# MoE blocks of 32 tokens on four 32-column strips in a two-layer encoder trunk

## The chip, the cores and the metric

The kernel is one program on one core of a Trainium2 chip. The metric is device time in microseconds (us) from launch to end. All arithmetic is float32. Engines: TensorE (PE: matmuls; PEld: its weight loads), VectorE (DVE), ScalarE (ACT), GpSimd (POOL), SyncE (SP, which issues most DMAs here).

## What is computed

The reference is a trunk of two layers on 256 tokens of width 1024: a convolution mixer, then an attention mixer. After each mixer comes a layer norm and a mixture of experts (MoE). The change touches only the MoE, and so the rest is left out here. The reference's MoE, cut:

```python
logits = (t @ router_w) + router_b                     # t: 256 x 1024 tokens, 16 experts
probs = softmax(logits).reshape(N, 4, 4)               # 4 groups of 4 experts
g_sel = argmax(top_k(probs, 2)[0].sum(-1))             # one group for a token
w_top, i_top = top_k(probs of that group, 2)           # two experts of it
w_top = w_top / w_top.sum(-1)
...
y_block = (silu(xb @ w_gate[e]) * (xb @ w_up[e])) @ w_down[e]
...
out[token] += weight * y_block[slot]
```

Each of the three matrices of an expert is 1024 x 1024, 4 MB, so an expert has 12 MB, and the two layers 384 MB.

## The kernel before

The expert weights stream through a ring of eight slots of 2 MB. A slot holds half of a matrix (512 rows by 1024 columns); in the text a *half* is such a piece. `load` (L295 and on, its `dma_start` is L303) on SyncE issues half number `index` into slot `index % 8`, and waits before that until the semaphore `half_free` says that half `index - 8` has been released. `load_experts` issues six halves an expert, in the order gate 0, gate 1, up 0, up 1, down 0, down 1. The 16 experts are walked in four turns of a hardware loop; its body has the code of four experts (`UNROLL`), so that slot numbers are fixed in it.

The router (`moe` of VectorE) finds for each token its two experts and its place in each one's list, and for each expert the number of blocks, `blocks_i`. A block is `SLOTS` = 64 places of an expert's list. The engines read that number into a register and branch by it. Each engine has its own copy of the walk, and they meet at semaphores that count blocks (`n_pe`, `n_dve`, `n_act`).

A block goes through these steps:

- VectorE builds a 0/1 matrix G (tokens by slots, L1170) and the same with router weights, GW (L1173).
- TensorE gathers: `sum_x` (L747) multiplies G with the tokens `hs`. The 64 slots fill 64 columns of the array, so columns 0 to 511 of the tokens go on one strip of 64 columns and the rest on the other (`tile_position`), and the result is 128 x 512.
- ScalarE copies it (L455), `turn_x` transposes it (L759), VectorE copies it to XT (L1179).
- `product` (L770) multiplies with gate, then with up, then (in `down`) with the down matrix: 16 matmuls of 128x64 by 128x512 each time, alternating between two strips.
- ScalarE applies silu to the gate product (L459), as soon as that is there and while the up product runs; VectorE multiplies by up (L1184).
- `down` transposes the hidden block (L783) and GW (L789), ScalarE copies the first (L463), VectorE the second (L1188), then comes the down product; ScalarE copies its result (L466).
- `combine` (L801) multiplies with GW and adds to the sums of all tokens in PSUM banks 0 to 3.

`expert` writes three bodies: a loop for all but the last two blocks, the last block, and, within conditionals between the last one's steps, the block before it. Two buffers of everything let these two go side by side. `sum_x` of the following expert stands ahead of `combine`. Halves are released in pairs, with the first matmul after the product that used them, in the last block only. A shortened view of the last part:

```python
n = pe.snap(n_pe) + 1
turn_x(0, n)
with pe.If(blocks > 1): ...                      # block 1: sum_x, turn_x
product(gate_w, ...)                             # and block 1's
product(up_w, ..., frees 2)                      # and block 1's
down(0, n, down_w, turn, 2)                      # and block 1's, with its combine
sum_x(0, following, 2)
combine(0, n, 0)
```

## Time and profile before

| | us |
|---|---|
| runs, median of 3 | 1681.42 |
| runs, lowest and highest | 1673.98, 1688.25 |
| profiled execution, span | 1682.1 |
| first product of layer 0's experts to the last combine's end | 281.43 to 805.73 |
| the same of layer 1 | 1107.12 to 1662.11 |
| weights moved by SyncE's queue | 490.90 MB |

The runs are three timed executions of the same program. The profile is one more execution with the hardware profiler on; its times are what the sums are made from. The span is from its first to its last instruction. Every fp32 matmul stands in the profile as two records, each with its weight load; transposes are one record each. A busy share says how much of the time an engine had an instruction in work, not that it set the end; the chain of waits follows the work back from the last instruction.

### The profile page before, as it was taken

How to read it: one execution, taken by the hardware profiler on the slowest of the kernel's cores; microseconds unless marked ns; L12 is line 12 of the kernel's file. 1: busy time of each engine (PE TensorE's matmuls, PEld its weight loads, DVE VectorE, ACT ScalarE, POOL GpSimd, SP SyncE). 2: the span in 40 equal slices, each digit the busy share in tenths (PEclk: the TensorE clock that was granted, in tenths of full speed). 3: DMA queues.
4: the chain of work that ended last, by engine and by line, in shares of the span. 5: the costliest groups of instructions: out<-in, count | busy, mean ns of one | idle time of the engine just before them, and what ended most of it. 6: DMA issues, size and time to landing. Idle time of an engine off the chain costs nothing.

```text
span 1682.1 us, 16133 instructions
## 1 busy us (share of the span) xinstructions
PE 1416.4 (84%) x6244; PEld 628.7 (37%) x6245; DVE 342.6 (20%) x821; ACT 258.9 (15%) x426; POOL 56.8 (3%) x89
## 2 busy tenths in 40 slices
PE   2795889996998798798799999789969897997996
PEld 0574534332333233233367565333323332332332
DVE  0199242101001001001601331510101110100103
ACT  0104201121011121121100211111111111121121
POOL 0290000000000000000000000000000000000000
PEclk8797988998999899899899857689989998998997
DMA  9816666999599999999952502149967778999991
GB/s 338 337 74 277 250 252 263 409 408 371 200 350 409 360 409 408 381 409 413 411 206 101 200 1 84 66 165 408 408 247 276 303 279 320 381 408 405 383 408 45
DMA packets 119596, 497.12 MB, mean 296 GB/s; under 512 B 6396, under 2 KB 6396, under 8 KB 111270
## 3 DMA queue, kind: packets, MB, share of 16 engines
q1 hardware_dynamic: 115404, 490.90, 74.1%
q10 hardware_dynamic: 3930, 4.09, 0.8%
q8 instruction: 123, 2.02, 0.5%
q14 instruction: 11, 0.09, 0.0%
q0 software_dynamic: 128, 0.02, 0.0%
HBM read 493.94 MB, written 1.05 MB: 294 GB/s over the span
## 4 chain that ended last, share of the span: by engine, by line
PE 78%; DVE 11%; issue 6%; ACTq 3%; ACT 2%; DMA 1%; DVEq 0%; SPq 0%
PE PS L770 45%; PE PS L669 5%; PE PS L747 4%; PE PS L801 4%; DVE work L1248 3%; PE PS L687 3%; PE PS L900 2%; PE PS L604 2%; PE PS L759 1%; PE PS L975 1%; PE PS L885 1%; PE PS L978 1%; DVE work L1179 1%; PE PS L783 1%; ACTq L422 1%
## 5 line engine op out<-in xcount | busy, mean ns | idle before, releaser
L770 PE MATMUL PS<-ring,work 128*64 128x512 f32 x3360 | 750.4, 603 | 55.7 <-DVE work L1179 34.9
L770 PEld LDWEIGHTS PS<-ring,work 128*64 128x64 f32 x3360 | 253.3, 139 | 510.3 <-issue 489.5
L1184 DVE TENSOR_TENSOR work<-work,PS 128x512 f32<-128x512 f32 x35 | 24.1, 688 | 515.5 <-PE PS L770 515.5
L1179 DVE COPY work<-PS 128x512 f32<-128x512 f32 x35 | 24.2, 692 | 360.9 <-PE PS L759 360.9
L669 PE MATMUL PS<-ring,hT 128*128 128x512 f32 x192 | 84.8, 603 | 4.1 <-ACT hT L526 3.6
L747 PE MATMUL PS<-hs,work 128*64 128x512 f32 x280 | 73.4, 644 | 9.6 <-DVE work L1173 9.6
L1248 DVE SCALAR_TENSOR_TENSOR work<-work,colv 128x256 f32<-128x256 f32 x150 | 77.3, 576 | 1.1
L604 PE MATMUL PS<-ring,crep 128*32 128x512 f32 x448 | 62.5, 707 | 17.7 <-DMA ring<-in_w_ada_dram 15.9
L759 PE MATMUL PS<-ident,work 128*128 128x128 f32 x140 | 25.7, 312 | 59.3 <-issue 55.8
L801 PE MATMUL PS<-work 64*128 64x512 f32 x280 | 69.6, 615 | 3.6 <-ACT work L466 3.6
L459 ACT ACTIVATE work<-PS 128x512 f32<-128x512 f32 x35 | 20.9, 598 | 326.8 <-PE PS L770 326.8
L463 ACT ACTIVATE work<-PS 128x512 f32<-128x512 f32 x35 | 20.9, 597 | 268.4 <-PE PS L783 268.4
L885 PE MATMUL PS<-hT,ring 128*128 128x256 f32 x256 | 58.2, 392 | 4.7 <-ACT hT L432 4.7
L466 ACT ACTIVATE work<-PS 128x512 f32<-128x512 f32 x35 | 20.9, 598 | 255.7 <-PE PS L770 255.7
L687 PE MATMUL PS<-hT,ring 128*128 128x256 f32 x256 | 55.8, 380 | 1.9 <-DVE hT L1038 1.9
L669 PEld LDWEIGHTS PS<-ring,hT 128*128 128x128 f32 x192 | 36.9, 193 | 50.3 <-issue 49.6
L885 PEld LDWEIGHTS PS<-hT,ring 128*128 128x128 f32 x256 | 50.5, 198 | 12.4 <-ACT hT L432 5.1
L687 PEld LDWEIGHTS PS<-hT,ring 128*128 128x128 f32 x256 | 48.5, 190 | 9.4 <-DVE hT L1038 2.2
L759 PEld LDWEIGHTS PS<-ident,work 128*128 128x128 f32 x140 | 16.4, 153 | 89.5 <-issue 63.0
L455 ACT ACT_TABLE_LOAD x32 | 41.1, 1283 | 40.2 <-issue 30.6
L900 PE MATMUL PS<-work,hs 128*128 128x256 f32 x124 | 30.1, 408 | 19.4 <-DVE work L1234 19.4
L783 PE MATMUL PS<-ident,work 128*128 128x128 f32 x140 | 22.1, 281 | 27.6 <-DVE work L1184 27.6
(197 smaller groups left out, 895.0 us busy)
## 6 DMA issues: line engine op xcount, KB each, us to landing
ring<-in_w_gate_dram SPq DMA_DIRECT2D x64, 2048.0 KB, 16.8
ring<-in_w_up_dram SPq DMA_DIRECT2D x64, 2048.0 KB, 13.2
ring<-in_w_down_dram SPq DMA_DIRECT2D x64, 2048.0 KB, 16.4
ring<-in_w_ada_dram SPq DMA_DIRECT2D x24, 2048.0 KB, 20.3
ring<-in_w_pw_dram SPq DMA_DIRECT2D x6, 2048.0 KB, 41.3
ring<-in_w_ada_kv_dram SPq DMA_DIRECT2D x4, 2048.0 KB, 14.9
ring<-in_w_kvf_dram SPq DMA_DIRECT2D x4, 2048.0 KB, 21.9
ring<-in_w_q_dram SPq DMA_DIRECT2D x2, 2048.0 KB, 24.0
```

What stands on the lines that cost most here:

```text
L455: act.activation(Xg[b], PS[:, X_BANK[b], :], ACT.Copy).then_inc(X_copied, 1)
L604: last = pe.matmul(PS[32 * q:32 * q + 32, bank, :], crep[:, k, :], quarter(index + j, kk, 2)[:, q * BANK:(q + 1) * BANK], start=(k == 0), ...
L669: last = pe.matmul(PS[:, banks + 2 * t + q, :], hT[:, k, t * P:(t + 1) * P], quarter(index + h, kk, KH)[:, q * BANK:(q + 1) * BANK], start ...
L687: last = pe.matmul(PS[:, banks + f // 2, (f % 2) * SEQ:(f % 2 + 1) * SEQ], quarter(index + h, kk, KH)[:, f * P:(f + 1) * P], hT[:, k, :], ...
L747: last = pe.matmul(PS[SLOTS * q:SLOTS * (q + 1), X_BANK[b], :], G[b][:, t, :], hs[:, t, q * BANK:(q + 1) * BANK], start=(t == 0), stop=(t ...
L759: last = pe.transpose(PS[:, XT_BANK[b], cc * P:(cc + 1) * P], Xg[b][:, cc * P:(cc + 1) * P], ident[:, :])
L770: last = pe.matmul(PS[SLOTS * q:SLOTS * (q + 1), bank, :], stationary[:, kk, SLOTS * h:SLOTS * (h + 1)], quarter(load + h, kk, KH)[:, q * ...
L801: last = pe.matmul(PS[:, 2 * t + q, :], GWT[b][SLOTS * q:SLOTS * (q + 1), t * P:(t + 1) * P], yb[b][SLOTS * q:SLOTS * (q + 1), :], start=F ...
L885: last = pe.matmul(PS[:, f, g * SEQ:(g + 1) * SEQ], quarter(L_PW1 + j, kk, 2)[:, g * D + f * P:g * D + (f + 1) * P], hT[:, k, :], start=(k ...
L900: last = pe.matmul(PS[:, f, 0:SEQ], diag(n), U[:, f, j:j + SEQ], start=(j == 0), stop=(j == TAPS - 1))
L1179: dve.tensor_copy(XT[b].rearrange("p c s -> p (c s)"), PS[:, XT_BANK[b], :]).then_inc(XT_copied, 1)
L1248: ins = dve.scalar_tensor_tensor(out=CV[:, fc, :], in0=U[:, fc, j:j + SEQ], scalar=colv[:, fc, j:j + 1], in1=CV[:, fc, :], op0=ALU.mult, o ...
```

## The change

A block has 32 slots. The array has four strips of 32 columns, and the steps are laid out over them:

- `gate_up` puts gate's two halves of the columns on strips 0 and 1 and up's on strips 2 and 3, so that one pass of 32 matmuls does both. Gate lies in partitions 0 to 63 of bank 4, up in 64 to 127. Silu starts when both are done.
- `sum_x` gathers on four strips, a quarter of the token's columns each: 8 matmuls of 256 columns. Two transposes replace four.
- `down` puts even and odd row blocks of the down matrix on different strips; their two partial sums are added by `combine`, whose matmuls keep their shape, as GW holds its weights four times over.
- The gather of the next block (of the same expert or of the next) lies inside a block: `sum_x` behind `gate_up`, `turn_x` behind the transposes of the hidden block. The first gather of a layer stands ahead of the loop.
- There is one buffer of each, and one body per block. An expert with several blocks runs all but the last in a loop, and then the last.
- The loads of an expert go gate 0, up 0, gate 1, up 1, down 0, down 1. In the last block the first pair is released in the middle of `gate_up`, the second at the first transpose of GW, and the down halves one by one, in mid-product and with `combine`.
- The number of blocks is found with one comparison against eight limits and a sum.

```diff
+SLOTS = 32
+STRIPS = 4
 RING = 8
...
-        X_BANK, XT_BANK = (7, 5), (6, 4)
-        GATE_BANK, UP_BANK = (4, 6), (5, 7)
-        HT_BANK, GWT_BANK, DOWN_BANK = (4, 6), (5, 7), (5, 7)
+        GU_BANK, X_BANK, GWT_BANK, HT_BANK, DOWN_BANK = 4, 5, 6, 7, 4
...
-                        for m, w in enumerate((gate_h, up_h, down_h)):
-                            for h in range(2):
-                                load(index + 6 * i + 2 * m + h,
-                                     w[bass.ds(e, 1), h].rearrange("o p k f -> (o p) k f"), turn * TURN)
+                        for m, (w, h) in enumerate(((gate_h, 0), (up_h, 0), (gate_h, 1), (up_h, 1),
+                                                    (down_h, 0), (down_h, 1))):
+                            load(index + 6 * i + m,
+                                 w[bass.ds(e, 1), h].rearrange("o p k f -> (o p) k f"), turn * TURN)
...
+                    act.activation(Xg, PS[:, X_BANK, 0:QUART], ACT.Copy).then_inc(X_copied, 1)
+
+                def gate(n):
+                    act.wait_ge(gate_up_done, n)
+                    act.activation(hh[64:P, :], PS[0:64, GU_BANK, :], ACT.Silu).then_inc(sil_ready, 1)
...
                 act.wait_ge(routed, l + 1)
+                take_x(act.snap(n_act) + 1)
...
+                    with act.If(blocks > 1):
+                        with act.Fori(0, blocks - 1):
                             n = act.snap(n_act) + 1
-                            take_x(0, n)
-                            gate(0, n)
-                            take_result(0, n)
+                            gate(n)
+                            take_x(n + 1)
+                            take_result(n)
                             act.reg_add(n_act, n_act, 1)
...
-                        for q in range(2):
-                            last = pe.matmul(PS[SLOTS * q:SLOTS * (q + 1), X_BANK[b], :], G[b][:, t, :],
-                                             hs[:, t, q * BANK:(q + 1) * BANK], start=(t == 0),
+                        for q in range(STRIPS):
+                            last = pe.matmul(PS[SLOTS * q:SLOTS * (q + 1), X_BANK, 0:QUART], G[:, t, :],
+                                             hs[:, t, q * QUART:(q + 1) * QUART], start=(t == 0),
...
+                def gate_up(n, load, turn, frees):
+
+                    pe.wait_ge(XT_copied, n)
+                    for h in range(2):
+                        arrived(load + 2 * h, turn)
+                        arrived(load + 2 * h + 1, turn)
+                        for kk in range(KH):
+                            q, cc = 2 * h + kk // 2, kk % 2
+                            for strip in range(STRIPS):
+                                half = strip % 2
+                                last = pe.matmul(PS[SLOTS * strip:SLOTS * (strip + 1), GU_BANK, :],
+                                                 XT[:, cc, SLOTS * q:SLOTS * (q + 1)],
+                                                 quarter(load + 2 * h + strip // 2, kk, KH)[:, half * BANK:(half + 1) * BANK],
+                                                 start=(h == 0 and kk == 0), stop=(h == 1 and kk == KH - 1),
+                                                 tile_position=(0, SLOTS * strip), skip_group_check=True)
+                        if h == 0 and frees:
+                            last.then_inc(half_free, 2)
+                    last.then_inc(gate_up_done, 1)
+
+                def turn_gw_await_hh(n, frees):
+
+                    pe.wait_ge(GW_built, n)
+                    for t in range(TT):
+                        if t == TT - 1:
+                            pe.wait_ge(hh_ready, n)
+                        last = pe.transpose(PS[:, GWT_BANK, t * P:(t + 1) * P],
+                                            GW[:, t, :, :].rearrange("p r s -> p (r s)"), ident[:, :])
+                        if frees and t == 0:
+                            last.then_inc(half_free, 2)
+                    last.then_inc(GW_turned, 1)
+
+                def turn_hh(n):
...
                     for cc in range(KH):
...
+                        last = pe.transpose(PS[:, HT_BANK, cc * 2 * SLOTS:(cc + 1) * 2 * SLOTS],
+                                            hh[64:P, cc * P:(cc + 1) * P], ident[64:P, 64:P])
+                    last.then_inc(hh_turned, 1)
...
+                def down(n, load, turn, frees):
+
+                    pe.wait_ge(hhT_copied, n)
                     for h in range(2):
...
+                            for half in range(2):
+                                strip = 2 * half + kk % 2
+                                last = pe.matmul(PS[SLOTS * strip:SLOTS * (strip + 1), DOWN_BANK, :],
+                                                 hhT[:, kk, SLOTS * h:SLOTS * (h + 1)],
+                                                 quarter(load + 4 + h, kk, KH)[:, half * BANK:(half + 1) * BANK],
+                                                 start=(h == 0 and kk < 2), stop=(h == 1 and kk >= KH - 2),
+                                                 tile_position=(0, SLOTS * strip), skip_group_check=True)
+                        if h == 0 and frees:
+                            last.then_inc(half_free, 1)
+                    last.then_inc(down_done, 1)
...
+                                             GWT[64 * q:64 * (q + 1), t * P:(t + 1) * P],
+                                             yb[64 * q:64 * (q + 1), :], start=False, stop=False,
...
                             if frees and t == q == 0:
-                                last.then_inc(half_free, frees)
...
+                                last.then_inc(half_free, 1)
...
+                def expert(load, turn, blocks, closes_turn):
+
+                    with pe.If(blocks > 1):
+                        with pe.Fori(0, blocks - 1):
                             n = pe.snap(n_pe) + 1
-                            turn_x(0, n)
-                            product(gate_w, turn, GATE_BANK[0], XT[0], gate_done, 0)
-                            product(up_w, turn, UP_BANK[0], XT[0], up_done, 0)
-                            down(0, n, down_w, turn, 0)
-                            sum_x(0, n + 1, 0)
-                            combine(0, n, 0)
+                            gate_up(n, load, turn, False)
+                            sum_x(n + 1)
+                            turn_gw_await_hh(n, False)
+                            turn_hh(n)
+                            turn_x(n + 1)
+                            down(n, load, turn, False)
+                            combine(n, False)
                             pe.reg_add(n_pe, n_pe, 1)
...
+                    gate_up(n, load, turn, True)
                     if closes_turn:
                         with pe.If(turn < E // UNROLL - 1):
-                            sum_x(0, following, 0)
-                        combine(0, n, 2)
+                            sum_x(n + 1)
                     else:
-                        sum_x(0, following, 2)
-                        combine(0, n, 0)
+                        sum_x(n + 1)
+                    turn_gw_await_hh(n, True)
+                    turn_hh(n)
+                    if closes_turn:
+                        with pe.If(turn < E // UNROLL - 1):
+                            turn_x(n + 1)
+                    else:
+                        turn_x(n + 1)
+                    down(n, load, turn, True)
+                    combine(n, True)
+                    pe.reg_add(n_pe, n_pe, 1)
 
                 pe.wait_ge(routed, l + 1)
-                sum_x(0, pe.snap(n_pe) + 1, 0)
+                first = pe.snap(n_pe) + 1
+                sum_x(first)
+                turn_x(first)
...
-                link(dve.tensor_scalar(r_n[:, :], cnt, float(SLOTS), 1.0, ALU.is_gt, ALU.add))
-                for m in range(2, SEQ // SLOTS):
-                    dst = r_n if m < SEQ // SLOTS - 1 else blocks_i
-                    link(dve.scalar_tensor_tensor(out=dst[:, :], in0=cnt, scalar=float(m * SLOTS), in1=r_n[:, :],
-                                                  op0=ALU.is_gt, op1=ALU.add))
+                NB = SEQ // SLOTS
+                limits = slot1[0:1, SLOTS - 1:SLOTS - 1 + SEQ].rearrange("o (m s) -> o m s", s=SLOTS)[:, :, 0]
+                link(dve.tensor_tensor(r_over[:, :, :], cnt.unsqueeze(2).to_broadcast([1, E, NB]),
+                                       limits.unsqueeze(1).to_broadcast([1, E, NB]), ALU.is_gt))
+                link(dve.tensor_reduce(r_n[:, :], r_over[:, :, :], AX.X, ALU.add))
+                link(dve.tensor_scalar(blocks_i[:, :], r_n[:, :], 1.0, None, ALU.max))
...
+                def build_G(e, end_slot):
+
                     for t in range(TT):
-                        dve.tensor_scalar(G[b][:, t, :], slots, r_pos[:, t, bass.ds(e, 1)], None, ALU.is_equal)
+                        last = dve.tensor_scalar(G[:, t, :], slots_of(end_slot), r_pos[:, t, bass.ds(e, 1)], None,
+                                                 ALU.is_equal)
+                    last.then_inc(G_built, 1)
...
+                def build_GW(e, end_slot):
...
+                        last = dve.tensor_scalar(GW[:, t, :, :], slots, r_pos[:, t, bass.ds(e, 1)],
+                                                 r_wn[:, t, bass.ds(e, 1)], ALU.is_equal, ALU.mult)
+                    last.then_inc(GW_built, 1)
...
+                    dve.tensor_tensor(hh[64:P, :], hh[64:P, :], PS[64:P, GU_BANK, :], ALU.mult).then_inc(hh_ready, 1)
...
+                build_G(0, SLOTS)
+                build_GW(0, SLOTS)
+                take_xT(dve.snap(n_dve) + 1)
...
+                    with dve.If(blocks > 1):
+                        with dve.Fori(0, blocks - 1) as j:
                             n = dve.snap(n_dve) + 1
-                            build(0, e, (j + 1) * SLOTS)
-                            take_xT(0, n)
-                            times_up(0, n)
-                            take_weights(0, n)
+                            build_G(e, (j + 2) * SLOTS)
+                            times_up(n)
+                            take_weights(n)
+                            take_xT(n + 1)
+                            build_GW(e, (j + 2) * SLOTS)
                             dve.reg_add(n_dve, n_dve, 1)
...
+                    with dve.If(e < E - 1):
+                        build_G(e + 1, SLOTS)
+                    times_up(n)
+                    take_weights(n)
+                    with dve.If(e < E - 1):
+                        take_xT(n + 1)
+                        build_GW(e + 1, SLOTS)
                     dve.reg_add(n_dve, n_dve, 1)
```

How this moves instructions, first on TensorE: the last block of an expert, with what stands in conditionals between its steps, before (L759 and L747 the gather, L770 the products; "x" is the number of instructions):

```order
L759 MATMUL PS<-ident,work 128x128 x4
L826 COMPARE_AND_BRANCH
L744 REGISTER_ALU
L747 MATMUL PS<-hs,work 64x512 x4
L759 MATMUL PS<-ident,work 128x128 x4
L826 UNCONDITIONAL_BRANCH
L587 ISA
L770 MATMUL PS<-ring,work 64x512 x16
L830 COMPARE_AND_BRANCH
L770 MATMUL PS<-ring,work 64x512 x16
L830 UNCONDITIONAL_BRANCH
L770 MATMUL PS<-ring,work 64x512 x16
```

and the same place now (L768 `gate_up`, L744 the gather of the next block, L783 GW, L792 the hidden block, L754 the next gather's transposes, L804 `down`, L819 `combine`):

```order
L840 ISA
L584 ISA
L768 MATMUL PS<-ring,work 32x512 x32
L741 REGISTER_ALU
L744 MATMUL PS<-hs,work 32x256 x8
L783 MATMUL PS<-ident,work 128x128 x2
L792 MATMUL PS<-ident,work 128x64 x4
L754 MATMUL PS<-ident,work 128x128 x2
L804 MATMUL PS<-ring,work 32x512 x16
L819 MATMUL PS<-work 128x512 x4
L856 ISA
```

The conditional copies between the products are gone, one pass of 32 matmuls stands where two of 16 stood, and the gather lies between it and `down`. The loop ahead of it, now run for every block but the last:

```order
L830 ISA
L584 ISA
L768 MATMUL PS<-ring,work 32x512 x32
L741 REGISTER_ALU
L744 MATMUL PS<-hs,work 32x256 x8
L783 MATMUL PS<-ident,work 128x128 x2
L792 MATMUL PS<-ident,work 128x64 x4
L754 MATMUL PS<-ident,work 128x128 x2
L804 MATMUL PS<-ring,work 32x512 x16
L819 MATMUL PS<-work 128x512 x4
L838 ISA
L829 COMPARE_AND_BRANCH
```

Its backward branch stands behind `combine`. The same on SyncE, the six loads of the first expert of a turn (REGISTER_ALU computes the value to wait for), before:

```order
L303 DMA ring<-in_w_gate_dram 128x4x1024
L301 REGISTER_ALU
L303 ISA
L303 DMA ring<-in_w_gate_dram 128x4x1024
L301 REGISTER_ALU
L303 DMA ring<-in_w_up_dram 128x4x1024
L301 REGISTER_ALU
L303 DMA ring<-in_w_up_dram 128x4x1024
L301 REGISTER_ALU
L303 DMA ring<-in_w_down_dram 128x4x1024
L301 REGISTER_ALU
L303 DMA ring<-in_w_down_dram 128x4x1024
```

and now:

```order
L305 DMA ring<-in_w_gate_dram 128x4x1024
L303 REGISTER_ALU
L305 DMA ring<-in_w_up_dram 128x4x1024
L303 REGISTER_ALU
L305 ISA
L305 DMA ring<-in_w_gate_dram 128x4x1024
L303 REGISTER_ALU
L305 DMA ring<-in_w_up_dram 128x4x1024
L303 REGISTER_ALU
L305 DMA ring<-in_w_down_dram 128x4x1024
L303 REGISTER_ALU
L305 DMA ring<-in_w_down_dram 128x4x1024
```

The first up half has moved ahead of the second gate half; their number and size are the same. On ScalarE silu now stands ahead of the copy of a gather, which is that of the next block; it has half the partitions.

## Rows read from the trace of the kernel before

**Rows 1.** The head of the page: span, busy time and share of each engine.

```profile
span 1682.1 us, 16133 instructions
...
PE 1416.4 (84%) x6244; PEld 628.7 (37%) x6245; DVE 342.6 (20%) x821; ACT 258.9 (15%) x426; POOL 56.8 (3%) x89
```

**Rows 2.** Chain of waits in order of time: start us, us, engine, line, records.

```profile
281.43 15.67 PE PS L770 x64
...
414.67 29.38 PE PS L770 x128
...
497.82 13.98 PE PS L770 x64
514.13 7.09 PE PS L770 x32
521.22 1.72 PE PS L747 x8
522.93 1.92 PE PS L801 x8
526.48 13.98 PE PS L770 x64
...
553.65 9.29 issue
565.21 15.72 PE PS L770 x64
...
803.74 1.99 PE PS L801 x8
...
1107.12 15.67 PE PS L770 x64
...
1660.12 1.99 PE PS L801 x8
```

**Rows 3.** Groups by line: busy us, mean ns | idle before; VectorE's product, then GW.

```profile
L1184 DVE TENSOR_TENSOR work<-work,PS 128x512 f32<-128x512 f32 x35 | 24.1, 688 | 515.5 <-PE PS L770 515.5
...
L1173 DVE TENSOR_SCALAR work<-slot,r_pos,r_w 128x64 f32 x140 | 34.3, 311 | 0.0
```

**Rows 4.** Windows: busy of PE, PEld, DVE, ACT, POOL; then clock, DMA share, GB/s.

```profile
308.00:396.00 88.00, 80.07 (x376) 29.14 (x374) 9.34 (x27) 16.59 (x20) 0.00 (x0) 1.00 1.03 408
420.00:430.00 10.00, 10.00 (x50) 3.42 (x46) 0.00 (x0) 0.60 (x1) 0.00 (x0) 1.00 0.01 2
36.00:60.00 24.00, 12.10 (x56) 4.78 (x56) 6.84 (x7) 0.00 (x0) 0.00 (x0) 0.64 1.03 408
```

**Rows 5.** Timeline, TensorE's four-strip adaLN product, full and low clock.

```profile
176.18 7.07 PE L604 MATMUL PS<-ring,crep 128*32 128x512 f32 x64
...
29.80 3.42 PE L604 MATMUL PS<-ring,crep 128*32 128x512 f32 x16 [3.93 <-DMA ring<-in_w_ada_dram]
```

**Rows 6.** Timeline, hand-offs around down, combine, and a router product.

```profile
483.23 0.69 DVE L1184 TENSOR_TENSOR work<-work,PS 128x512 f32<-128x512 f32 x1 [14.48 <-PE PS L770]
...
484.06 0.63 PE L783 MATMUL PS<-ident,work 128*128 128x128 f32 x4 [0.95 <-DVE work L1184]
...
484.73 0.60 ACT L463 ACTIVATE work<-PS 128x512 f32<-128x512 f32 x1 [7.84 <-PE PS L783]
484.95 0.42 DVE L1188 COPY work<-PS 128x256 f32<-128x256 f32 x1 [1.03 <-PE PS L789]
...
461.65 1.99 PE L801 MATMUL PS<-work 64*128 64x512 f32 x8 [0.69 <-ACT work L466]
...
255.66 2.52 PE L713 MATMUL PS<-rw,hT 128*128 128x16 f32 x21 [0.78 <-DVE hT L1038]
```

**Rows 7.** SyncE's issues by time, then issue to landing for 425 to 470 us.

```profile
270.31 3.08 SPq L303 DMA_DIRECT2D ring<-in_w_gate_dram  x2
...
431.20 0.92 SPq L303 DMA_DIRECT2D ring<-in_w_up_dram  x2
...
DMA to landing us min/median/max: 7.9/10.8/13.8
```

162 lines of the change are left out of this document (42 added, 120 removed).

## The prediction

> **What bounds the kernel now.** I read the page's head first: a span of 1682.1 us, and TensorE with something to do for 84% of it [rows 1]. That share does not say which stage TensorE holds back, so the chain of waits in order of time comes next [rows 2]. It shows the two MoE stages, 281 to 805.7 us (803.74 plus 1.99) and 1107 to 1662.1 us, built almost wholly of TensorE work. A one-block expert repeats every 28.66 us (497.82 to 526.48): 13.98 for gate and up, 7.09 for down, 1.72 for the next gather, 1.92 for the combine, and 3.95 of hand-offs and transposes. After every fourth expert the loop turns back and the chain has 9.29 us of "issue"; from the last combine to the next gate product pass 11.56 us (553.65 to 565.21) where it is 1.63 otherwise (524.85 to 526.48), so a turn costs 9.8 to 9.9; I take 9.8. The first product after it takes 15.72 instead of 13.98, 1.7 more. There are 35 blocks over the 32 experts of the two layers [rows 3].
>
> The DMA side is nearly as full. Where one-block experts run undisturbed the queue moves 408 GB/s at a share of 1.03 and TensorE's clock is 1.00; inside the two-block expert at 414.67 the queue moves 2 GB/s, since all ring slots wait to be released [rows 2, 4]. A half of a weight is 2.097 MB, so it costs 2.097/0.408 = 5.14 us and an expert's six 30.8 us. That is more than 28.66: TensorE keeps its pace only because the DMA queue catches up in the turns. So a faster block cannot gain more than the DMA's slack.
>
> **The new block.** Count its matmuls: 32 for gate and up, 16 for down, 8 narrow ones for the gather, 4 for the combine, 8 transposes (16, 16, 16, 4, 4, and 10 before). Each fp32 matmul is two records. On two strips 64 records take 13.98 us; on four 32-column strips the adaLN product does 64 in 7.07 [rows 2, 5]. So gate with up is 7.0 and down 3.5. The combine stays 1.92.
> Between gate_up and down: ScalarE's silu 0.60, VectorE's product 0.69, three hand-offs of 0.1 to 0.15 (483.23 + 0.69 to 484.06, say), then five short transposes at 0.63 for four, and a copy of 256 columns, 0.42 on VectorE, with 0.15 around it [rows 6]: 1.65 + 0.75 + 0.57 = 3.0, and I take 3.1 because ScalarE copies the next gather ahead of it. The gather of the next block and its two transposes lie in this gap. The gather is 16 records of half the columns: 0.9 us at the adaLN rate, 2.0 at the rate of the small router products, which 21 records at 2.52 us show [rows 6]; silu and product cover 1.65, so it adds nothing or up to 0.4. What is late there if it is longer is the transpose of the hidden block. Down to combine is 0.69, with a copy of 0.60 between [rows 6]. In sum 7.0 + 3.1 + 3.5 + 0.7 + 1.9 = **16.2 us per block**; bounds 15.7 (less cover needed) and 18.
>
> The number of blocks follows from the reference's router on its drawn inputs. Of at most 32 tokens each, layer 0 has one block per expert but three for expert 4 and two for experts 5, 6, 10, 11, 15: 23 for 17 now. Layer 1 has the same with three for expert 6: 24 for 18. The two stages take 524 + 555 = 1079 us now. TensorE's work in them falls to 47 x 16.2 and six turns of 9.8, 820 us, under the 987 us that 192 halves cost. The stages become bound by the DMA queue, and by what the ring makes it wait.
>
> **The sum.** Rules: a half lands 5.14 us after the one before. If the ring was full, 3.6 us pass between the release and the start: two halves issued into an idle queue landed 7.9 and 13.8 us after their issue, that is 2 x 5.14 + 3.5 [rows 7]. An expert's first release comes 3.5 us into its last block, 12.7 before its end. The ring has room for two halves beyond an expert in work. After a turn or a long wait a block takes 1.7 more.
> Layer 0 begins its first product at 280.5 (281.43 now [rows 2]; the first gather is shorter by 1 to 2.5). Halves 6 and 7, issued at 270.31, land by 288.1 [rows 7]. Half 23 lands at 288.1 + 16 x 5.14 = 370.3, expert 3 ends 4.4 later (half of down, copy, combine), and with the turn expert 4 begins at 384.5. Its three blocks cost 3 x 16.2 + 2 x 1.7 + 3.1 (its last halves are late) + 5 for the loop back, explained below: it ends at 444.7 and first releases at 432.0. The last two halves with room, up to 31, landed at 411.5: the DMA pauses 20.5 us. From then no pause: half 95 lands at 432.0 + 3.6 + 64 x 5.14 = 764.5, and what is left is 4.4 and one whole block: **785.1 against 805.7, -20.6**.
> Layer 1 (in its own times of now) starts with a full ring at 1105, first release 1110.2. Half 23 lands at 1113.8 + 82.2 = 1196.0; expert 4 runs 1210.2 to 1270.4, releases at 1257.7; expert 5 takes 32.4, expert 6 48.6 + 5 + 1.7, to 1358.1, releases at 1345.4, a second pause of 22.4. Half 95 lands at 1345.4 + 3.6 + 52 x 5.14 = 1616.3, the end is 20.6 later: **1636.9 against 1662.1, -25.2**. Sum -45.8. The same rules, given the blocks of now, end at 806.4 and 1661.9.
> The profiled execution has 1682.1 us, the median of the runs 1681.4: 1682.1 - 45.8 = 1636.
>
> **Edits costed at nothing.** The order gate, up, gate, up of the loads and the earlier releases (two halves in mid-product) are in the rules. G and GW are built by VectorE in four steps of about 0.31 us [rows 3] while TensorE does 7 us of products. The load of silu's table stands on ScalarE ahead of silu, after the block's last copy, beside combine and products. The test of the block count is one step shorter. What stands outside the MoE is untouched.
>
> **What the trace does not show: the loop inside an expert.** Now its body never runs, since no expert has three blocks of 64. Its backward branch will be taken three times. The nearest row is the turn, 9.3 us [rows 2]; the lower end is nothing, since the body is about an eighth of a turn. I take 5, the middle. At nothing the total is -66, at 9.3 it is -33. All of it is on the path: TensorE is late then, and the ring full.
> The Trainium skill, "Runtime: NRT & Kernel Launch", section "Instruction fetch mechanics", says that a taken branch out of the pages at hand stalls for a fetch. The turn's 9.29 us agree; no row here shows whether the short jump leaves those pages. By that rule read strictly the sum is the -33 case, 1649.
>
> **Rivals.**
> A. Loop backs at full price, as above: 1649. For: it is the nearest row. Against: the body is short.
> B. No loop-back cost: 1616.
> C. The block is longer than 16.2, through a hand-off that I cannot see. One us more on each block costs 29 us, since it delays the multi-block experts and lengthens the pauses: 1665, no change to speak of. For: in the new gap ScalarE and VectorE work in turns, with branches between their steps. Against: most of these branches fall under products.
> D. Slower: every run of the loop body, 15 in all, stalls TensorE as the turn does, not only the three loop backs. Place: between the blocks of an expert, with its six slots held. At 9.3 each the total is +108, 1790; it is slower than now from about 2 us each, with 1.7 more for the clock. Against: the 128 records of products at 414.67, half of them from conditional bodies, run now in one piece of 29.38 us [rows 2].
> E. The clock stays low. In 36 to 60 us, where TensorE waits for weights, the granted clock is 0.64 and 16 records of the four-strip product take 3.42 us instead of 1.77 [rows 4, 5]. One-block experts at half speed need 16.2 + 12.4 = 28.6 us and stay under 30.8, so it costs nothing there. If it stayed so through the first 25 us after each wait the total is +2; a return after 3 to 14 us leaves -46. The row at 565.21 shows it back within the product.
> The Trainium skill, "TensorE: Matmul & The Clock Gate", section "HAM oscillation — how this bites in real kernels", says that a kernel whose matmuls wait for each slice of weights starts every slice at the low clock. By it the one-block experts show a clock well under 1.00, and the sum stays, as they have the time.
> F. The change does nothing, because the DMA was the bound already: 1682. Against: without pauses layer 0 would end at 288.1 + 452.3 + 20.6 = 761, 45 us before it does now.
>
> **How the numbers follow.** My forecast with its own spread (rate 5.00 to 5.28 us per half: -55 to -23; loop back 0 to 9.3) 55%, B's end 15%, A 10%, C 11%, D 5%, E 3%, F 1%. Range 1598 (B with the faster rate and 15.8 us per block) to 1675. A measurement of this kernel can tell about 1% (17 us) from no change. Faster by over 1%: forecast, B, A, half of C, 0.82. Within 1%: the rest of C, F, part of E, 0.10. Slower: D and what is left, 0.08.
>
> **What would show it.** Right: 64 gate-up records in 7.0 us, 32 down in 3.5, blocks in multi-block experts every 16 to 17 us; waits of TensorE on the ring's DMA, which are absent now; the DMA at 408 GB/s but for one gap in layer 0 and two in layer 1 of about 20 us; TensorE's clock and busy share lower. Wrong: no waits on the ring, blocks of 18 us or more, issue gaps between an expert's blocks, or a rate per record over 0.12 us at the full clock.

## The result, and where the time went

| | before | after |
|---|---|---|
| runs, median | 1684.84 (the three of the earlier table and one more) | 1628.93 (4 runs, 1627.07 to 1653.75) |
| ratio | | 0.968, 95% interval 0.9623 to 0.9736 |
| profiled execution, span | 1682.1 | 1625.2 |
| first gate product of layer 0 | 281.4 | 283.4 |
| layer 0's experts, first product to last combine | 524.3 | 513.6 |
| from there to layer 1's first gate product | 301.4 | 279.4 |
| layer 1's experts | 555.0 | 528.9 |
| from there to the end | 20.0 | 19.9 |

The prediction was 1636; the kernel measured 1628.93, faster by 3.2%. The ratio is formed without the run of 1653.75, in which TensorE's granted clock was lower than in the other three (0.863 against 0.876 to 0.887). The stages of the two profiles add up to 56.9 us: +2.0 ahead of layer 0, -10.7 in it, -22.0 between the two, -26.1 in layer 1. So the experts' stages gave -36.8, where -45.8 was predicted (3 of it from earlier starts), and -22.0 came from a stretch whose code is the same in both kernels and where nothing was predicted. The total was met by luck: one term was too large and one was missing.

The head of the page of after, which answers to [rows 1], and its shares of the chain:

```profile
span 1625.2 us, 19834 instructions
...
PE 1247.7 (77%) x7990; PEld 530.1 (33%) x7991; DVE 351.9 (22%) x835; ACT 244.7 (15%) x457; POOL 56.7 (3%) x89
...
PE 47%; DMA 33%; DVE 8%; issue 4%; ACT 3%; ACTq 3%; SPq 2%; DVEq 0%
```

There are more instructions, TensorE's share falls from 84% to 77%, and a third of the chain is now DMA. (In the chain a DMA piece is a load from its issue to its landing. TensorE works through most of that time and waits only for its end.) The chain of waits of after in order of time, which answers to [rows 2] (start us, us, engine, line, records):

```profile
283.38 9.12 PE PS L768 x64
...
309.12 24.86 DMA ring<-in_w_up_dram
...
349.71 25.41 DMA ring<-in_w_down_dram
...
409.69 1.99 PE PS L819 x8
411.68 7.05 PE PS L768 x64
421.31 3.69 PE PS L804 x32
425.67 1.99 PE PS L819 x8
427.66 7.00 PE PS L768 x64
436.40 19.42 DMA ring<-in_w_down_dram
...
460.50 7.00 PE PS L768 x64
...
509.30 4.85 issue
...
532.93 10.30 issue
...
794.95 1.99 PE PS L819 x8
...
1076.33 8.55 PE PS L768 x64
...
1603.27 1.99 PE PS L819 x8
```

The three-block expert of layer 0 shows the new block undisturbed: 64 records of gate and up in 7.05 us, down in 3.69, the combine in 1.99, and 15.98 from block to block (411.68 to 427.66). The backward jump of the loop inside an expert lies ahead of the second of its three blocks, and the chain has no gap at it: 409.69 + 1.99 is 411.68. Nor has it one where the loop is left: 425.67 + 1.99 is 427.66. Elsewhere the chain runs through the loads, 19 to 25 us each, of up and of down halves. TensorE itself waits for a few microseconds at a time. Its waits for expert weights over the whole execution (us in total, times, longest):

```profile
PE PS L768 <- DMA ring<-in_w_up_dram: 139.8, 29, 6.1
...
PE PS L804 <- DMA ring<-in_w_down_dram: 14.5, 19, 2.0
```

That is 154 us in 48 waits, where the experts of the kernel before have none.

Windows of after, beside [rows 4] (busy of PE, PEld, DVE, ACT, POOL; then clock, DMA share, GB/s): the one-block experts of layer 0, the last blocks of the three-block expert, and 50 us of layer 1's attention.

```profile
308.00:396.00 88.00, 55.89 (x382) 18.11 (x374) 7.60 (x21) 9.70 (x15) 0.00 (x0) 0.84 1.03 408
415.00:430.00 15.00, 13.87 (x124) 4.66 (x120) 2.44 (x7) 3.23 (x5) 0.00 (x0) 1.00 0.03 10
...
941.00:991.00 50.00, 50.00 (x260) 30.85 (x253) 23.13 (x88) 12.56 (x53) 0.00 (x0) 0.95 0.16 61
```

In the first row the queue is as full as before (408 GB/s, share 1.03) and TensorE busy for 56 of 88 us where it was 80. In the second the ring is full of weights in use and the queue stands still.

**The stretch between the layers.** Of the -22.0 us, 19.4 lie in layer 1's attention, from the end of the q product to the start of the next large weight product (106.2 before, 86.8 after). Fifty microseconds of that stretch in before:

```profile
960.00:1010.00 50.00, 50.00 (x159) 32.09 (x160) 15.25 (x58) 8.94 (x35) 0.00 (x0) 0.57 0.00 1
```

TensorE has something in work for all 50 us in both. At a granted clock of 0.57 it gets through 159 records, at 0.95 through 260. (The two windows lie 34 and 24 us into the stretch; its last 50 us have 170 and 259 records.) So these 19.4 us are the clock's, and the experiments have to say whether the change owns them.

### The profile page after: what moved, and what is told of

It is laid out like the page before. It is cut to its first block, busy times and chain, and to the rows that moved or that the text cites. A ratio compares the mean times of both kernels' runs of the same rounds, so it can differ in the third digit from the quotient of the medians.

```text
span 1625.2 us, 19834 instructions
## 1 busy us (share of the span) xinstructions
PE 1247.7 (77%) x7990; PEld 530.1 (33%) x7991; DVE 351.9 (22%) x835; ACT 244.7 (15%) x457; POOL 56.7 (3%) x89
## 4 chain that ended last, share of the span: by engine, by line
PE 47%; DMA 33%; DVE 8%; issue 4%; ACT 3%; ACTq 3%; SPq 2%; DVEq 0%
DMA ring<-in_w_down_dram 24%; PE PS L768 13%; DMA ring<-in_w_up_dram 9%; PE PS L804 6%; PE PS L666 5%; PE PS L819 4%; DVE work L1264 3%; PE PS L684 3%; PE PS L601 3%; PE PS L910 2%; SPq L305 2%; PE PS L895 1%; ACTq L424 1%; ACT work L468 1%; PE PS L988 1%
## 5 line engine op out<-in xcount | busy, mean ns | idle before, releaser
L768 PE MATMUL PS<-ring,work 128*32 128x512 f32 x3008 | 406.7, 691 | 195.3 <-DMA ring<-in_w_up_dram 139.8
L768 PEld LDWEIGHTS PS<-ring,work 128*32 128x32 f32 x3008 | 112.4, 125 | 482.9 <-issue 481.6
L1201 DVE TENSOR_TENSOR work<-work,PS 64x512 f32<-64x512 f32 x47 | 32.5, 691 | 848.2 <-ACT work L461 848.2
L804 PE MATMUL PS<-ring,work 128*32 128x512 f32 x1504 | 178.6, 606 | 21.1 <-DMA ring<-in_w_down_dram 14.5
L461 ACT ACTIVATE work<-PS 64x512 f32<-64x512 f32 x47 | 27.6, 588 | 619.8 <-PE PS L768 619.8
L819 PE MATMUL PS<-work 64*128 64x512 f32 x376 | 93.4, 615 | 33.7 <-ACT work L468 33.7
L804 PEld LDWEIGHTS PS<-ring,work 128*32 128x32 f32 x1504 | 42.8, 111 | 125.2 <-issue 77.6
L819 PEld LDWEIGHTS PS<-work 64*128 64x128 f32 x376 | 32.4, 186 | 98.5 <-ACT work L468 76.4
L468 ACT ACTIVATE work<-PS 128x512 f32<-128x512 f32 x47 | 28.1, 597 | 199.7 <-PE PS L804 199.7
L684 PE MATMUL PS<-hT,ring 128*128 128x256 f32 x256 | 55.8, 380 | 1.9 <-DVE hT L1048 1.9
L744 PE MATMUL PS<-hs,work 128*32 128x256 f32 x752 | 53.3, 390 | 1.8 <-DVE work L1183 1.8
L895 PEld LDWEIGHTS PS<-hT,ring 128*128 128x128 f32 x256 | 50.0, 196 | 11.1 <-ACT hT L434 3.9
L783 PE MATMUL PS<-ident,work 128*128 128x128 f32 x94 | 30.9, 329 | 16.2 <-DVE work L1201 16.2
L744 PEld LDWEIGHTS PS<-hs,work 128*32 128x32 f32 x752 | 26.9, 112 | 37.3 <-issue 27.4
## 6 DMA issues: line engine op xcount, KB each, us to landing
ring<-in_w_up_dram SPq DMA_DIRECT2D x64, 2048.0 KB, 23.5
ring<-in_w_ada_dram SPq DMA_DIRECT2D x24, 2048.0 KB, 20.6
ring<-in_w_kvf_dram SPq DMA_DIRECT2D x4, 2048.0 KB, 19.9
```

Source lines behind the costliest of these rows:

```text
L461: act.activation(hh[64:P, :], PS[0:64, GU_BANK, :], ACT.Silu).then_inc(sil_ready, 1)
L468: act.activation(yb, PS[:, DOWN_BANK, :], ACT.Copy).then_inc(yb_copied, 1)
L684: last = pe.matmul(PS[:, banks + f // 2, (f % 2) * SEQ:(f % 2 + 1) * SEQ], quarter(index + h, kk, KH)[:, f * P:(f + 1) * P], hT[:, k, :], ...
L744: last = pe.matmul(PS[SLOTS * q:SLOTS * (q + 1), X_BANK, 0:QUART], G[:, t, :], hs[:, t, q * QUART:(q + 1) * QUART], start=(t == 0), stop=( ...
L768: last = pe.matmul(PS[SLOTS * strip:SLOTS * (strip + 1), GU_BANK, :], XT[:, cc, SLOTS * q:SLOTS * (q + 1)], quarter(load + 2 * h + strip / ...
L804: last = pe.matmul(PS[SLOTS * strip:SLOTS * (strip + 1), DOWN_BANK, :], hhT[:, kk, SLOTS * h:SLOTS * (h + 1)], quarter(load + 4 + h, kk, K ...
```

## The experiments

All ratios are to runs of the kernel before beside them (medians 1687.1 to 1689.3), with the 95% interval. Stage lengths come from the one profile of each run, layer 0 and then layer 1; where a difference is given without its base, the base is the profile of after (513.6 and 528.9).

**Both kernels again.** No edit.

> The kernel before, unchanged, for its attention stage. In the profile of before the stretch from the end of the query projection to the start of the output projection takes 106 us with a granted clock of 0.67, in the profile of after 87 us at 0.86, though its code is the same in both. Theory (the clock of that stretch varies from execution to execution): this run shows another value than 106, anywhere from 85 to 106, and the total moves with it, 1662 to 1682. Rival (the change sets it, by when the stage begins or by what runs ahead of it): 106 again, within 1, and a total within 3 of 1682.

> The changed kernel, unchanged. Theory: the two MoE stages repeat within 2 us (513.5 and 529.0 from first product to last combine), and the attention stretch may take anything from 85 to 106 us, the total moving with it. Rival: 87 again within 1 us, in the profile and in the total of 1627.

Before: 1692.25 us, 1.0038 [0.9991, 1.0085]; stages 524.2 and 555.5, attention 106.2. After: 1636.55, 0.9778 [0.9701, 0.9854]; stages 513.5 and 528.2, attention 85.7. So the gain is 2.2% here and was 3.2% there, and the interval of this repeat reaches up to 0.985. The stages repeat within a microsecond, which makes one profile enough to compare them. The attention repeated too, within 1.1 us, which is nearer to the rivals than to the theories.

But it is not a mark of the two kernels. The changed kernel cut to one block (below) had 106.3 and the old kernel with an unrolled loop 89.8. Over all readable profiles it took 85.7 to 86.8 (the change twice, two blocks), 89.8 (four kernels), 97.0 and 97.3 (two), 106.2 to 106.3 (the kernel before twice, one block) and 110.7 (two strips by order). Nor is it an accident of the profiled executions: the medians of the two repeats differ by 55.7 us and their stages by 37.9, so some 18 us lie outside the stages in the timed runs as well. What decides this clock stays open; no experiment here was made for it. For the runs below it means that a total says less than the stages do.

**One block per expert**, which leaves out the tokens past an expert's 32nd:

```diff
-link(dve.tensor_scalar(blocks_i[:, :], r_n[:, :], 1.0, None, ALU.max))
+link(dve.tensor_scalar(blocks_i[:, :], r_n[:, :], 1.0, 1.0, ALU.max, ALU.min))
```

> The changed kernel with every expert held to one block: tokens beyond the first 32 of an expert are left out, the weights are all still loaded. Theory (the DMA queue bounds the stages, and only experts with several blocks make it pause): 192 halves at 5.25 us, no pause: each stage 474 us from first product to last combine, 40 and 55 us less than with the change; no pause of the DMA over 3 us. Rival (TensorE's work and its turns bound them): 15 blocks fewer would only give 7 or 8 times 16 us a stage, 385 to 400 us, the loads following.

1541.36 us, 0.9185 [0.9073, 0.9297]; stages 472.3 and 472.7. The window over the first of them shows what sets it:

```profile
282.70:755.00 472.30, 298.10 (x2031) 94.67 (x2031) 39.10 (x107) 50.31 (x79) 0.00 (x0) 0.83 1.02 408
```

408 GB/s over the whole of it, TensorE busy for 298 of 472 us. That is the floor that 96 halves set, less what the ring held at the start. What the change has above it, 41 us in layer 0 and 56 in layer 1, comes with the experts of several blocks; the windows of the last part show it as time in which the ring is held and the queue stands.

**At least two blocks per expert** (`ALU.max` with 2.0, where 1.0 stood):

> The changed kernel with at least two blocks for every expert (the second one empty where there was one; the result stays). That adds 10 blocks a layer, all to one-block experts. Theory (recurrence with measured lengths: blocks of 16, halves of 5.25, released only in an expert's last block): TensorE becomes the bound nearly everywhere, stages of 570 and 586 us, 56 to 57 more each, a third of the 160 us that 10 blocks cost hidden in the waits there are now. Rival (the waits of one-block experts have room for a whole block, 25 us per block against 16): below 20 us more a stage. The opposite rival (nothing hides them): 160 us more a stage.

1730.37 us, 1.0311 [1.0227, 1.0396]; stages 565.7 and 584.0, as the theory had it. There are ten blocks more in each layer, and they cost 52.2 and 55.8 us over the 513.5 and 528.2 of the change's repeat: 5.2 to 5.6 us each, where a block is 16 long. Two thirds of the 160 us are hidden (the expectation has the right stages and says a third).

**The old order of loads**, with the release of the second pair moved to where both are free:

```diff
-for m, (w, h) in enumerate(((gate_h, 0), (up_h, 0), (gate_h, 1), (up_h, 1),
+for m, (w, h) in enumerate(((gate_h, 0), (gate_h, 1), (up_h, 0), (up_h, 1),
...
-                            last.then_inc(half_free, 2)
+                            last.then_inc(half_free, 1)
...
-                            last.then_inc(half_free, 2)
+                            last.then_inc(half_free, 3)
```

> The changed kernel with the loads in the old order, gate 0, gate 1, up 0, up 1; in mid-product only gate 0 can be released then, the other three at the first transpose of GW. Theory (the queue is the bound at 5.25 us a half and never runs dry for want of a release in a one-block expert): both stages the same within 4 us (513.5 and 528.5 now). Rival (the order and the release in mid-product are where the gain over the old kernel comes from): 10 us more a stage or above.

1640.22 us, 0.9722 [0.9647, 0.9798]; stages 520.4 and 533.0: +6.8 and +4.1 (theory at most 4, rival 10 or more). Layer 1 is at the theory's limit, layer 0 between the two. The order, with the releases that it allows, is worth some 5 us a stage.

**Release as late as can be**: nothing in mid-product, all four gate and up halves at the transpose of GW, both down halves with the combine.

```diff
-                        if h == 0 and frees:
-                            last.then_inc(half_free, 2)
...
-                            last.then_inc(half_free, 2)
+                            last.then_inc(half_free, 4)
...
-                        if h == 0 and frees:
-                            last.then_inc(half_free, 1)
...
-                                last.then_inc(half_free, 1)
+                                last.then_inc(half_free, 2)
```

> The changed kernel with its releases late: all four of gate and up at the first transpose of GW, both down halves with the combine, none inside a product. Theory (the queue's pauses lengthen by what the releases come later, after each expert with several blocks, and the one-block experts' releases now come too late as well): stages of about 534 and 550 us, 24 and 21 more than the recurrence gives the change. Rival (the ring is deep enough): within 4 us.

1686.28 us over 10 runs, 0.9983 [0.9942, 1.0024]; stages 542.2 and 557.6, 29 each over the change (theory +24 and +21). The total is back at that of before, but by two things that cancel: the stages are 18 and 3 us longer than before's 524.3 and 555.0, and the attention took 89.8 where it was 106.2. Its chain around the three-block expert:

```profile
412.89 7.05 PE PS L768 x64
...
428.87 7.00 PE PS L768 x64
...
438.86 22.55 DMA ring<-in_w_down_dram
...
468.61 7.37 PE PS L768 x64
```

The block is the same (412.89 to 428.87 is 15.98). But from its last block to the last block of the expert behind it pass 39.7 us (428.87 to 468.61), where it was 32.8 (427.66 to 460.50 in after), since the loads that wait for room start later. In layer 0 the two other places where an expert of several blocks follows another are 4.9 and 4.4 us longer, in layer 1 the three are 6.3, 4.1 and 4.4. That is 15 to 16 of the 29; the rest comes with the experts of one block. The few lines that say when a buffer is free are worth 57 us of stages, more than the 37 that the whole change brought.

**The gather late**: `sum_x` behind `down`, `turn_x` behind `combine`, and ScalarE's steps in that order.

> The changed kernel with the gather of the next block out of the gap: sum_x behind down, as before the change, its copy and transposes behind the combine. Theory: each block is longer by the gather's 0.9 us and by the transposes with the copy to XT, 1.3 us, so 18.2 instead of 16.0; only the blocks of experts with several count in full, and the stages take 534 and 552 us. Rival (one-block experts hide it and so do the copies): below 8 us a stage.

> The kernel with the gather behind down, once more, for a profile at the usual clock (in the one before every matmul ran at half speed, while the timed runs lay some 10 us above the change). Expected now: blocks of 17.5 to 18.2 us, and yet the stages only 3 to 8 us longer than with the change, since the experts with one block hide the rest.

The first of the two was profiled in an execution of 3036 us whose TensorE records were about 2.4 times as long as usual (a product 19.15 us), so its stages can't be read; its other four runs took 1635.5 to 1647.9, 0.9731 [0.9658, 0.9804]. The second: 1661.68 us (1638.51 to 1670.55); no interval; stages 523.0 and 539.4, +9.5 and +10.4, above the 3 to 8 expected. The chain shows the block:

```profile
412.28 7.11 PE PS L768 x64
...
421.97 3.64 PE PS L804 x32
425.61 0.86 PE PS L744 x16
426.48 1.92 PE PS L819 x8
428.39 0.38 PE PS L754 x2
...
429.24 0.23 issue
429.47 7.11 PE PS L768 x64
```

It is 17.2 us long, 1.2 over the change's and not the 2.2 expected. I had added the gather's 0.86 and all hand-offs behind it. But the gather falls into the 0.7 us in which `combine` waits for ScalarE's copy in any case and costs 0.2, and the two transposes and a copy (428.39 to 429.47) come on top. The stages are nearer to the first rival (below 8) than to the theory (some 20).

**Two strips, by order of the program**: within each half of the rows, first the eight matmuls of strips 0 and 1 (gate), then the eight of 2 and 3 (up); in `down` first the even row blocks, then the odd.

```diff
-                        for kk in range(KH):
+                        for kk, strip in [(k, 2 * m + s) for m in range(2) for k in range(KH) for s in range(2)]:
                             q, cc = 2 * h + kk // 2, kk % 2
-                            for strip in range(STRIPS):
+                            if True:
...
-                        for kk in range(KH):
+                        for kk in (0, 2, 1, 3):
```

> The changed kernel with the same blocks of 32 and the same matmuls, but ordered so that only two of the four strips are in work at any time: gate first, then up, and in down the even row blocks first, then the odd. Theory (four strips side by side are what halves the products): gate_up 14 instead of 7 us, down 7.1 instead of 3.7, blocks of 26.4 us, stages of 645 and 672 us, slower than before the change by 8 to 10%. Rival (the strips overlap anyway, since each record has its own strip and the queue looks ahead): block and stages as in the change.

1661.58 and 1688.89 us (two runs, no interval; the profile is of the second); stages 534.4 and 546.8 where 645 and 672 were expected. The theory fell: the block is 17.8 us, not 26.4, at a granted clock of 1.00. TensorE's weight loads in time order, and then the matmuls at the end of the product (L744 is the gather behind it):

```profile
432.39 0.14 PEld L768 LDWEIGHTS PS<-ring,work 128*32 128x32 f32 x4 [0.76 <-issue]
...
433.27 0.12 PEld L768 LDWEIGHTS PS<-ring,work 128*32 128x32 f32 x2 [0.31 <-issue]
433.70 0.12 PEld L768 LDWEIGHTS PS<-ring,work 128*32 128x32 f32 x2 [0.31 <-issue]
434.13 0.15 PEld L768 LDWEIGHTS PS<-ring,work 128*32 128x32 f32 x6 [0.31 <-issue]
434.56 0.15 PEld L768 LDWEIGHTS PS<-ring,work 128*32 128x32 f32 x4 [0.28 <-issue]
...
439.40 0.63 PE L744 MATMUL PS<-hs,work 128*32 128x256 f32 x4
439.82 1.03 PE L768 MATMUL PS<-ring,work 128*32 128x512 f32 x4
440.26 0.63 PE L744 MATMUL PS<-hs,work 128*32 128x256 f32 x4
440.68 0.60 PE L768 MATMUL PS<-ring,work 128*32 128x512 f32 x2
```

Two strips at work take two records in 0.43 us. From 434.13 on there are four on average, although the program has no instruction of strips 2 and 3 until the eight matmuls of strips 0 and 1 (16 records) stand, and only 10 of these (4, 2, 2 and 2) had their weights loaded before 434.13. At the end matmuls of the gather start ahead of products that precede them in the program. So a matmul on a free strip starts while earlier ones of other strips still stand. The order in the program matters less than the strips named.

**Two strips in truth**: gate and up both on strips 0 and 1, in two banks (silu and its neighbours read the new places); `down` and the gather stay on four.

```diff
-                                last = pe.matmul(PS[SLOTS * strip:SLOTS * (strip + 1), GU_BANK, :],
+                                last = pe.matmul(PS[SLOTS * half:SLOTS * (half + 1), (GU_BANK, HT_BANK)[strip // 2], :],
...
-                                                 tile_position=(0, SLOTS * strip), skip_group_check=True)
+                                                 tile_position=(0, SLOTS * half), skip_group_check=True)
...
```

> The changed kernel with gate and up on the same two strips (0 and 1), in two PSUM banks, so that a strip has twice the matmuls and strips 2 and 3 have none in this product; down and gather stay on four. Theory, after the run in which strips that only stood apart in program order still overlapped: a strip works its own matmuls one after another, so gate_up takes 13.8 us instead of 7.05, a block 22.7, and the stages 586 and 610 us, 10% longer than before the change for 47 blocks against 35. Rival (the rate is set by the records, 0.11 us each, whatever strip they are on): as in the change.

1781.62 us (two runs), 1.0552 [1.0468, 1.0637]; stages 588.2 and 602.1 (586 and 610 expected). Its timeline around a block:

```profile
437.43 13.50 PE L768 MATMUL PS<-ring,work 128*32 128x512 f32 x62
...
453.95 3.64 PE L804 MATMUL PS<-ring,work 128*32 128x512 f32 x32
458.31 1.99 PE L819 MATMUL PS<-work 64*128 64x512 f32 x8 [0.72 <-ACT work L468]
460.23 2.34 PE L768 MATMUL PS<-ring,work 128*32 128x512 f32 x10
```

62 of the records in 13.50 us, and 22.8 from block to block (437.43 to 460.23), as the theory had it. With gate and up on two strips, blocks of 32 tokens would have been 5.5% slower than before: the four strips are worth 148 us of stages, and without them there is no change to make.

**No turns of the loop**: `UNROLL` 16 in place of 4, so that a layer's experts stand once in the program; first in the kernel before, then in the changed one.

```diff
-    UNROLL = 4
+    UNROLL = 16
```

> The kernel before with the code of all 16 experts in the loop's body, so that it never turns back; nothing else. Theory (before the change TensorE's pace and the turns set the stages, the DMA queue has slack of some 30 us a stage and only that can be had): with 28.66 us an expert and no 9.8 at the turns the queue becomes the bound here too; the stages take 497 and 522 us instead of 524 and 555, total about -61, as much as the change brings or more. Rival (the turns are hidden, or unrolling costs fetches of its own): less than 20 us in all.

> The changed kernel with the code of all 16 experts in the loop's body. Theory (after the change the turns fall into the queue's slack): the recurrence gives no change at all, stages of 513.5 and 528.5 within 4 us. Rival (the turns behind experts with several blocks, at 533 and 669 us, are on the path): up to 10 us less a stage.

The kernel before with this edit alone: 1621.39 us (1615.03 to 1624.75), 0.9591 [0.9531, 0.9651]; stages 500.8 and 529.6, attention 89.8. The changed one with it: 1623.53 us (1617.86 to 1629.70), 0.9606 [0.9561, 0.965]; stages 513.2 and 522.8. The old kernel's window over the same 88 us as in [rows 4]:

```profile
308.00:396.00 88.00, 80.32 (x378) 29.62 (x376) 9.33 (x27) 14.86 (x18) 0.00 (x0) 1.00 1.03 408
```

The blocks are as they were. The three turns a layer are gone, and there are three new gaps of up to 3.9 us in the whole execution. From TensorE's waits in it:

```profile
PE PS L759 <- issue: 11.1, 3, 3.9
...
PE PS L770 <- DMA ring<-in_w_down_dram: 0.6, 1, 0.6
```

The stages are 23.5 and 25.4 us shorter. That is as much as the whole change gives in layer 1, and 13 us more than it gives in layer 0. The total fell by a little more than the 61 expected (65.7 in the medians), but the stages by 49 and not by 60; another 16.4 us are the attention's. The theory had the queue as the new bound. It did not become that: TensorE waited for an expert's weights 0.6 us in all.

On top of the change the same edit gives 0.4 and 6.1 us: most of its turns had been hidden in waits for weights already (theory: within 4; rival: up to 10, which layer 1 is nearer to). Both of these versions are faster than the kernel before and, by their intervals, not slower than the change; which of the two is better these runs can't say. Both stages together are 1079.3 us before, 1042.5 with the change, 1030.5 with the turns gone and 1036.0 with both.

## Why the prediction was right, and where it wasn't

**What held.** The bound. The forecast was that the experts' stages pass from TensorE to the DMA queue, with pauses where an expert of several blocks holds the ring. The queue runs at 408 GB/s, and where 152 us went off TensorE's busy time in the stages (930.8 to 778.3), 37 came off their length. Cut to one block the stages go to the DMA's floor (472, against 474 expected) and not to that of TensorE. F (DMA was the bound already) fell with the 3.2%, though it was nearer than I saw: the floor of 472 and 41 for the held ring are not far below 524.

**The block** was put at 16.2 and measured 15.98: 7.05 for 7.0, 2.6 for 3.1 to the down product, 3.69 for 3.5, 0.7 and 1.99. Hiding the gather in the hand-off was right, and worth 1.2 us a block. C (17.2 and more) did not occur.

**The loop back inside an expert**, put at 5 (bounds 0 and 9.3), costs nothing in any of its three places. That was B's condition, and A fell. With the three jumps at 0 the prediction's own rules give 780.2 and 1626.9 for the ends of the layers, -61 and not the -66 that it prints (1621 and not 1616), so 58 us off the stages' lengths. 37 came. The 6 us by which the stages fall short of the forecast (43) are a gap of 21, most of it hidden by the 15 that the three jumps were priced at. D (a stall at each of the 15 runs of the loop's body) fell as well, at the three-block expert: blocks of 15.98 without an issue gap. New gaps did come elsewhere: 4.85 us at 509.30, ahead of an expert whose loop is skipped, and 2.37 at 304.13, in mid-product. They cost nothing that the windows show: TensorE waits for loads again behind both (3.12 us ahead of 323.88, 4.55 ahead of 572.88), and from 500 to 540 us the queue moves 410 GB/s.

**Layer 0's end** is the step that failed, by its size: 796.9 where 785.1 was forecast, so 8.8 before the old time and not 20.6. The rate was right: 408 GB/s over the one-block run's whole stage is 5.14 us for a half. The long pause was nearly so. It was forecast from 411.5 to 432.0 and 3.6 more. The window reads 18.4 us at 40 GB/s up to the release at 431.4, a pause of 16.6 that began some 3 us late, and 324 GB/s behind it, which is 1.8 us lost. What was wrong came after "From then no pause". Windows of after:

```profile
413.00:431.40 18.40, 17.27 (x156) 5.63 (x152) 2.44 (x7) 3.23 (x5) 0.00 (x0) 1.00 0.10 40
431.40:440.00 8.60, 8.18 (x84) 3.02 (x80) 2.53 (x7) 1.35 (x3) 0.00 (x0) 1.00 0.85 324
460.00:480.00 20.00, 18.87 (x168) 6.12 (x168) 2.53 (x7) 3.23 (x5) 0.00 (x0) 1.00 0.94 368
480.00:500.00 20.00, 18.20 (x164) 5.74 (x156) 2.44 (x7) 3.23 (x5) 0.00 (x0) 1.00 0.96 366
620.00:640.00 20.00, 18.86 (x168) 6.09 (x164) 2.54 (x7) 3.23 (x5) 0.00 (x0) 1.00 0.90 348
640.00:660.00 20.00, 18.13 (x165) 5.88 (x160) 2.44 (x7) 3.42 (x6) 0.00 (x0) 1.00 0.96 369
431.40:764.30 332.90, 247.45 (x1920) 79.94 (x1912) 37.60 (x105) 48.52 (x75) 0.00 (x0) 0.89 1.00 395
```

Two-block experts follow one another at 460 and at 620. Each takes 32.8 us (from last block to last block, 427.66 to 460.50) while its loads take 30.8, so the ring fills and the queue stops for a moment: against 409 GB/s the four windows lose 2.0, 2.1, 3.0 and 2.0 us, 9 in sum. Less what the restart and the earlier release gave (1.8 and 0.6), these are between 6 and 7 us. The second part is a lag: half 93 was to be the 62nd behind the pause, and TensorE got it at 764.34 (the second half of its product, after the last wait for up in layer 0), by when 395 x 332.9 is 131.5 MB, 62.7 halves. The forecast has that half at 754.3, 10.1 us earlier. So with several loads in the queue this one wasn't finished when its own bytes had gone by count; they seem to run side by side, which no run here tests. That is 3.6 us, an estimate from these two numbers, which I could not see in [rows 7], since the queue was idle there. The small stops are then 6.5 of the 10.1. The last 1.7 are the last block's down product at a lower clock (5.38 against 3.69). 6.5 + 3.6 + 1.7 is the 11.8 that the end is late. The gain of the loop back did not show here: the expert that has it began 1.4 us later than in my sum and took 25.8 instead of 21.0 for its first block, as its halves lagged too, and so its first release came at 431.4, close to the 432.0 forecast. One error hid the other. (The expectations above were worked with 5.25 us for a half, which swallows the lag and fits the ends; the windows show that it was not the rate.)

**Layer 1** was given 531.9 from its first product (1105.0 to 1636.9) and took 528.9. Its two pauses, 20.6 and 22.4 by the forecast's rules, are about 16 us each (20.4 us at 81 GB/s and 20.5 us at 84 GB/s), since the loop back has no price and blocks are 0.2 shorter. With the two jumps free the rules give 521.9, so 7 us are missing here and 14 in layer 0. The same small stops stand behind its experts of several blocks (318 GB/s from 1252 to 1261 us), but what each is worth in this layer was not worked out. The stage is 26.1 shorter where the forecast had 23.1 (25.2 with the start), by errors that largely cancel.

**The clock (E).** TensorE's granted clock in the waiting stretch is 0.84, and a product after a wait takes 9.12 us where it is 7.05, but the block still ends within the time of its loads. The sum did not change by it. The Trainium skill, "TensorE: Matmul & The Clock Gate", section "HAM oscillation — how this bites in real kernels", has a kernel that waits for each slice of weights begin every slice at the low clock. The 0.84 against 1.00 before agrees. What I did not see is the other side: the clock outside the experts. "What stands outside the MoE is untouched" is true of the code, and the attention's clock still moved by 19.4 us. The executions of the kernel before in its own repeat lie 23 us apart (1676.31 at a mean clock of 0.916, 1699.08 at 0.903), so an execution brings a term of this size by itself, and it belonged into the range. But the medians differ by some 18 us outside the stages as well, with this change and with the unrolled old kernel alike, so that what sets the clock there is a cause that these runs don't name.

**The reason for the gain** in the stages is shown from several sides. With gate and up on two strips they are 111 us longer than before, and with late releases 20, so the change needs both the four strips and the early releases. With the turns gone from both kernels they are 1030.5 us in the old one and 1036.0 in the new one: the new block then gives nothing, though the two are held by different things, the old one by TensorE (0.6 us of waits for the ring) and the new one by its loads. What the change gives is that TensorE catches up after a turn, so that the turns no longer count. That is 37 of the 57 us. The other 20 lie outside the experts, 19.4 of them at the attention's clock, and their cause is open.

## What to carry to other kernels

Where weights stream through a ring, work out first the time of the transfers alone (here 472 us a stage) and what holds the ring full beyond it. A faster product is worth only the difference, and a cheaper edit may reach it too: here an unrolled loop did what the new block did, and the time at which a buffer is released was worth more than the whole change (57 us of stages against 37). In a chain of waits, read a load's piece as its whole way and look up separately how long the engine waited for it. And a stretch isn't constant because its code is: where TensorE is busy throughout, look at its granted clock. Two kernels are then compared by their stages, as two totals can agree by chance.

## What the hardware showed that was not expected

- Matmuls on different column strips overlap across the order of the program: with strips 0 and 1 ahead of 2 and 3 in groups of eight matmuls the block was 17.8 us, against 15.98 with the strips in turn and 22.8 with gate and up on two strips alone.
- A taken branch has no one price. The jump back over one block cost 0 and the turn of the outer loop 10.3 to 11.1 us (9.2 to 9.5 before). Where an expert's loop is skipped there was a gap of 4.9 us ahead of one expert, in both executions of the change, and none that shows ahead of the others, where TensorE often waited for a load in any case; two of 2.2 to 2.4 us stood within a product. The Trainium skill, "Runtime: NRT & Kernel Launch", section "Instruction fetch mechanics", says that a branch out of the pages at hand stalls for a fetch. The 0 us of the short jump and the 10.3 or more of the longest are in keeping with it; which pages are at hand at a jump no run here shows.
- TensorE can have work for 50 us on end at a granted clock of 0.57 in one kernel's execution and of 0.95 in another's, with the same code in the stretch, which then takes 106 or 87 us. What lowers it is open.
- A load in a queue with others behind it was finished 0.7 of a half (3.6 us, an estimate from one place) later than the bytes that the queue had moved would give.
